# Head of a hybrid diffusion layer: modulation columns in two groups, first token block's features in two groups of four

## What is computed

```python
mod = jnp.dot(jax.nn.silu(cond), w_ada) + b_ada
sh1, sc1, gt1, sh2, sc2, gt2 = [m[:, None, :] for m in jnp.split(mod, 6, axis=-1)]
h = _rmsnorm(x, g_pre_mix) * (1 + sc1) + sh1
z = jnp.einsum('bld,de->ble', h, w_in)
q, k, v, o, ig, fg, u, ga, gb = jnp.split(z, IN_SPLIT_POINTS, axis=-1)
```

## Time and profile before

| | |
|---|---|
| median of 3 runs | 1746.36 us (1746.0 to 1747.34) |
| the profiled execution | 1746.76 us |
| its span | 1744.9 us |
| TensorE busy | 1728.8 us, 99% |
| VectorE, ScalarE, GpSimd busy | 1201.5, 680.1, 266.4 us |
| TensorE's granted clock over the span | 0.997 of full |

### The profile page before, as it was taken

The page is one execution under the profiler, slowest core; times in us unless marked ns, Lnnn a source line. Parts: engine busy times, 40 slices in busy tenths (PEclk is TensorE's granted clock), DMA queues, the critical chain, the costliest instruction groups (busy, mean ns, idle before and its releaser), DMA issues.

```text
span 1744.9 us, 26886 instructions
## 1 busy us (share of the span) xinstructions
PE 1728.8 (99%) x10432; PEld 1626.5 (93%) x10432; DVE 1201.5 (69%) x2547; ACT 680.1 (39%) x1229; POOL 266.4 (15%) x260
## 2 busy tenths in 40 slices
PE   8999999999999999999999999999999999999998
PEld 2998999999999999999988899999999999888887
DVE  4677556566565565364464579888888888798998
ACT  3633221333144143262243454434344444444454
POOL 3010000100000000010000062444433333100000
PEclk9999999999999999999999999999999999999999
DMA  9124334424434455265232331233222222686876
GB/s 346 52 56 141 90 105 128 126 84 145 112 95 159 124 138 185 74 243 170 95 125 94 105 121 66 86 114 110 90 71 72 75 76 76 199 279 221 272 248 246
DMA packets 216275, 236.17 MB, mean 135 GB/s; under 512 B 11568, under 2 KB 160828, under 8 KB 216148
## 3 DMA queue, kind: packets, MB, share of 16 engines
q1 hardware_dynamic: 200916, 179.54, 33.8%
q0 software_dynamic: 10752, 38.00, 6.4%
q10 hardware_dynamic: 4480, 16.91, 2.4%
HBM read 181.49 MB, written 52.92 MB: 134 GB/s over the span
## 4 chain that ended last, share of the span: by engine, by line
PE 90%; DVE 5%; ACT 1%; DMA 1%; issue 1%; SPq 1%; POOL 1%; ACTq 0%; DVEq 0%; POOLq 0%
PE ps L1466 19%; PE ps L1106 13%; PE ps L1107 12%; PE ps L1108 12%; PE ps L1408 6%; PE ps L1483 5%; PE ps L1484 5%; PE ps L1485 5%; PE ps L1273 2%; PE ps L1277 2%; PE ps L1275 2%; PE ps L1289 2%; PE ps L1291 1%; PE ps L1290 1%; DVE mid_g L2647 1%; DVE up_lo L2178 1%
## 5 line engine op out<-in xcount | busy, mean ns | idle before, releaser
L1106 PE MATMUL ps<-H_hi,ring_hi 128*128 128x384 f32 x1200 | 406.5, 339 | 4.7 <-DVE H_lo L2178 4.7
L1107 PE MATMUL ps<-H_lo,ring_hi 128*128 128x384 f32 x1200 | 401.9, 335 | 0.0
L1108 PE MATMUL ps<-H_hi,ring_lo 128*128 128x384 f32 x1200 | 401.8, 335 | 0.0
L1106 PEld LDWEIGHTS ps<-H_hi,ring_hi 128*128 128x128 f32 x1200 | 226.0, 188 | 5.8 <-DVE H_lo L2178 5.5
L1107 PEld LDWEIGHTS ps<-H_lo,ring_hi 128*128 128x128 f32 x1200 | 226.0, 188 | 0.3
L1108 PEld LDWEIGHTS ps<-H_hi,ring_lo 128*128 128x128 f32 x1200 | 225.8, 188 | 0.0
L2355 DVE SCALAR_TENSOR_TENSOR Cst<-Cst,GE,ps 128x257 f32<-128x257 f32 x56 | 26.8, 478 | 163.2 <-PE ps L1277 163.2
L1466 PE MATMUL ps<-T_hi,up_hi 128*128 128x288 f32 x608 | 130.5, 296 | 0.4 <-ACT held_g L2013 0.3
L1466 PE MATMUL ps<-T_hi,up_lo 128*128 128x288 f32 x608 | 130.2, 296 | 0.0
L1466 PE MATMUL ps<-T_lo,up_hi 128*128 128x288 f32 x608 | 130.2, 296 | 0.0
L2178 DVE TENSOR_TENSOR up_lo<-up_raw,up_hi 128x512 fp32r<-128x512 f32 x114 | 89.6, 789 | 57.2 <-ACT up_hi L1971 57.2
(11 more groups left out here) (332 smaller groups left out, 3609.1 us busy)
## 6 DMA issues: line engine op xcount, KB each, us to landing
raw<-in_w_in_dram SPq DMA_DIRECT2D x44, 512.0 KB, 4.1
up_raw<-in_w_up_dram SPq DMA_DIRECT2D x38, 512.0 KB, 5.2
w_raw<-in_w_down_dram SPq DMA_DIRECT2D x66, 256.0 KB, 3.3
raw<-in_w_ada_dram SPq DMA_DIRECT2D x32, 512.0 KB, 5.5
X<-z_f SPq DMA_DIRECT2D x44, 256.0 KB, 3.9
GE<-z_gates SPq DMA_DIRECT2D x72, 128.0 KB, 4.1
w_sub<-in_w_down_dram SPq DMA_DIRECT2D x33, 256.0 KB, 4.0
z_w_diff<-w_raw SPq DMA_DIRECT2D x22, 256.0 KB, 2.5
```

What stands on the lines that cost most here:

```text
L1106: pe.matmul(out, whi, xhi, start=first, stop=False)
L1107: pe.matmul(out, whi, xlo, start=False, stop=False)
L1108: return pe.matmul(out, wlo, xhi, start=False, stop=last)
```

## The change

- `w_ada` columns come as four rows of 512: row 0 is the shift and row 1 the scale of features 0 to 3, rows 2 and 3 those of features 4 to 7. They lie in the memory of `H_hi` and `H_lo`.
- SP's order: first token block, row 0, query unit, row 1 (in four parts), two value units, rows 2 and 3, token blocks 1 and 2. The eleven vectors are issued by ScalarE.
- All eight matmuls of each row are TensorE's. Rows 0 and 1 stand ahead of the first features. TensorE then does four query steps, row 2, the first four value steps of tiles 0 and 1, row 3, two transposes, the columns, the first four value steps of tile 2, four query steps, and the other twelve value steps. The last eight of these take the transposes of the second block.
- Four banks are open at a time: query, and a value tile each in banks 1, 2 and 6. The transposes of the first block have two banks (3 and 4), those of the others three (3, 4, 5).
- The low part of the query unit is VectorE's; the value units' high parts are ScalarE's and their low parts VectorE's. GpSimd has none of them.
- ScalarE evacuates value tile 1 behind the second block's features.

The core of the diff; left out are helper functions renamed or moved, the index of `first_coef` by group, and the loops of blocks 1 and 2, which are as before.

```diff
-    AG = ADA0 * P // 512
-
-    DVE_GROUP, PE_CELLS = 2, 2
-    DVE_CELLS = KD - PE_CELLS
-    ADA_PARTS = (1, 2, 2, 4)
+    FG = 2
+    KG = KD // FG
+    RW = KG * P
+    ADA_PARTS = (1, 4, 2, 2)
...
+    ada_at = [0, 0] + [BW + RW * (g - 1) if FG > 2 else T - RW for g in range(1, FG) for _ in range(2)]
+    ada_home = [place(f"ada_home{s}", [P, KD, T], at=HH0 + 4 * KD * T * s) for s in range(2)]
...
+    def ada_cols_of(r):
+
+        return slice((r % 2) * DM + r // 2 * RW, (r % 2) * DM + (r // 2 + 1) * RW)
+
+    def ada_rows_in(r, ks):
+
+        return ada_home[r % 2][:, ks, ada_at[r]:ada_at[r] + RW]
+
+    def row_out(r):
+
+        return ps[0:2, r % 2 if r < 2 else 5, 0:RW] if RW == 512 or r < 2 else ps[0:2, 5, r % 2 * RW:(r % 2 + 1) * RW]
+
+    def xt_bank(w):
+
+        return 3 + w % 2 if w < KD else 3 + w % 3
...
-            ada_load(0)
-            x_load(0)
-            ada_load(1)
...
-            ada_load(2)
-            ada_load(3)
...
+            x_load(0)
+            ada_load(0)
             for n, it in enumerate(raw_items):
+                if n == 1:
+                    ada_load(1)
                 if n == 3:
+                    for r in range(2, 2 * FG):
+                        if r == 2 * FG:
+                            x_load(1)
+                        ada_load(r)
...
-            hi1, lo1 = split_of(1)
-            pool.tensor_tensor(lo1, raw[:, raw_n(1) % RS, :], hi1, ALU.subtract).then_inc(lo_ready, 1)
-            v_raw, v_hi, v_lo = [[value_part(j, what) for j in range(2)] for what in ("raw", "hi", "lo")]
-            for j in range(2):
-                n = raw_n(2 + j)
-                pool.wait_ge(landed[n % RS], 16 * (n // RS + 1))
-                pool.tensor_copy(v_hi[j], v_raw[j]).then_inc(hi_ready, 1)
-                pool.wait_ge(hi_ready, 2 + j)
-                pool.tensor_tensor(v_lo[j], v_raw[j], v_hi[j], ALU.subtract).then_inc(lo_ready, 1)
...
+                if w >= 2:
+                    pe.wait_ge(xt_free, w - (1 if b == 0 else 2))
+                norm_turn(X0, ps[:, xt_bank(w), :], b, k).then_inc(xt_done, 1)
...
+            def ada_rows(r):
+
+                if r > 2 and (RW == 512 or r % 2 == 0):
+                    pe.wait_ge(row_read, r)
+                for k in range(KD):
+                    if k % (KD // ADA_PARTS[r]) == 0:
+                        pe.wait_ge(ada_part_in(r, k), 16)
+                    mm = pe.matmul(row_out(r), condT[:, :, k], ada_rows_in(r, k), start=(k == 0), stop=(k == KD - 1))
+                mm.then_inc(row_done, 1)
+
+            def ada_cols(group):
+
+                for r in (2 * group, 2 * group + 1):
+                    pe.wait_ge(row_read, r + 1)
+                    for j in range(KG):
+                        at = 2 * (r % 2 * KD + group * KG + j)
+                        mm = pe.transpose(ps[:, 7, at:at + 2], ada_row[:, r, j * P:(j + 1) * P], ident[0:2, 0:2])
+                mm.then_inc(ada_used, ADA0 // FG)
...
             pe.wait_ge(cond_done, 1)
             ada_rows(0)
-            ada_rows(1)
-            ada_rows(DVE_GROUP, 0, PE_CELLS, PE_CELLS)
             pe.wait_ge(vectors_in, 16 * 11)
             pe.transpose(ps[:, 7, 0:92], vecs[0:92, 0, :], ident[0:92, 0:92])
             pe.transpose(ps[:, 7, 92:180], vecs[0:88, 1, :], ident[0:88, 0:88])
             pe.transpose(ps[:, 7, 180:268], vecs[0:88, 2, :], ident[0:88, 0:88]).then_inc(vec_done, 1)
             pe.wait_ge(x_scaled, TB)
-            for k in range(4):
-                first_norm(0, k)
+            first_norm(0, 0)
+            first_norm(0, 1)
+            ada_rows(1)
             pe.wait_ge(vec_done, 2)
-            ada_cols(0, 0)
-            ada_cols(1, 8)
-            ada_rows(3, 0, 4)
-            ada_group_sum()
-            ada_cols(DVE_GROUP, 2 * ADA0).then_inc(ada_used, ADA0 // 2)
-            ada_rows(3, 4, KD)
-
-            for b in range(NB):
-                if b == 0:
-                    pe.wait_ge(lo_ready, 2)
+            ada_cols(0)
+
+            tiles_of = [[(j, k) for j in range(TB) for k in range(KG * g, KG * (g + 1))] for g in range(FG)]
+            turn_steps = tiles_of[FG - 1][-KD:]
+            turns = {step: range(KD * n // len(turn_steps), KD * (n + 1) // len(turn_steps)) for n, step in enumerate(turn_steps)}
+            for g in range(FG):
+                for k in range(KG * g, KG * (g + 1)):
+                    if k == 0:
+                        pe.wait_ge(lo_ready, 2)
+                    mm = ramp_query(0, k)
+                    if k + 2 < KD and (k + 2) // KG == g:
+                        first_norm(0, k + 2)
+                if g == FG - 1:
+                    mm.then_inc(done0, 1)
+                else:
+                    ada_rows(2 * g + 2)
+                for j, k in tiles_of[g]:
+                    if (j, k) == (0, 0):
+                        pe.wait_ge(lo_ready, 4)
+                    if j == TB - 1 and k == KG * g and g < FG - 1:
+                        ada_rows(2 * g + 3)
+                        for n in range(2):
+                            first_norm(0, KG * (g + 1) + n)
+                        ada_cols(g + 1)
+                    if g == FG - 1:
+                        for n in turns.get((j, k), ()):
+                            if n == 0:
+                                pe.wait_ge(x_scaled, 2 * TB)
+                            first_norm(1, n)
+                    mm = ramp_value(j, (1, 2, 6)[j], k)
+                    if k == KD - 1:
+                        mm.then_inc(done0, 1)
+
...
+            vecA = [b_ada[0], g_pre_mix[0], g_post_mix[0], g_pre_ffn[0], g_post_ffn[0],
+                    g_head[0].rearrange("h v -> (h v)"), pool_scale[0]]
+            at = 0
+            for v in vecA:
+                n = v.shape[0] // P
+                act.dma_start(vecs[at:at + n, 0, :], v.rearrange("(r p) -> r p", p=P)).then_inc(vectors_in, 16)
+                at += n
+            for j, o, v in ((1, 0, conv_w[0, 0]), (1, 44, conv_w[0, 1]), (2, 0, conv_w[0, 2]), (2, 44, conv_b[0])):
+                act.dma_start(vecs[o:o + 44, j, :], v.rearrange("(r p) -> r p", p=P)).then_inc(vectors_in, 16)
...
             hi_split(1)
+            row_copy(1)
             act.wait_ge(coef1, 1)
-            first_evac(0, range(0, 3))
+            first_evac(0, range(0, 2))
+            value_hi(0)
+            first_evac(0, range(2, 4))
+            value_hi(1)
+            row_copy(2)
             row_copy(3)
-            first_evac(0, range(3, 4))
             act.wait_ge(coef1, 2)
             first_evac(0, range(4, KD))
             x_stats(1)
             query_evac(0)
             value_evac(0)
+            first_evac(1)
             value_evac(1)
-            first_evac(1)
             value_evac(2)
...
             scale_x(0)
-            dve.wait_ge(cond_done, 1)
-            ada_group(PE_CELLS, KD)
+            lo_split(1)
             dve.wait_ge(vec_done, 2)
             first_coef(0)
...
-            norm_split(0, tsc, 4, 0, range(0, 3), direct=False)
+            norm_split(0, tsc, 4, 0, range(0, 2), direct=False)
+            value_lo(0)
+            norm_split(0, tsc, 4, 0, range(2, 4), direct=False)
+            value_lo(1)
             first_coef(1)
-            norm_split(0, tsc, 4, 0, range(3, KD), direct=False)
+            norm_split(0, tsc, 4, 0, range(4, KD), direct=False)
             scale_x(1)
             norm_split(0, tsc, 4, 1, direct=False)
             scale_x(2)
```

More of the change, by code:

```diff
@@ L512, in build @@
     staged = list(stage_no)
-    ROW_BANK = (0, 1, 2, 1)
     NORM_AFTER = (2, 5, 8)
@@ L1139, in first_norm @@
                 w = b * KD + k
-                if w >= 4:
-                    pe.wait_ge(xt_free, w - 3)
-                norm_turn(X0, ps[:, 3 + w % 4, :], b, k).then_inc(xt_done, 1)
-            def ada_rows(g, k0=0, k1=KD, last=KD):
-                if g == 3 and k0 == 0:
-                    pe.wait_ge(row_read, 2)
-                for k in range(k0, k1):
-                    if k % (KD // ADA_PARTS[g]) == 0:
-                        pe.wait_ge(ada_part_in(g, k), 16)
-                    mm = pe.matmul(ps[0:2, ROW_BANK[g], :], condT[:, :, k], adaw[:, g, k, :], start=(k == 0), stop=(k == last - 1))
-                if k1 == last:
-                    mm.then_inc(row_done, 1)
@@ L1156, in ada_cols @@
-            def ada_cols(g, at):
-                pe.wait_ge(row_read, g + 1)
-                for j in range(4):
-                    mm = pe.transpose(ps[:, 7, at + 2 * j:at + 2 * j + 2], ada_row[:, g, j * P:(j + 1) * P], ident[0:2, 0:2])
-                return mm
-            def ada_group_sum():
-                pe.wait_ge(ada_mac, 2 * DVE_CELLS)
-                pe.wait_ge(pool_seq, 7)
-                for a in range(4 * DVE_GROUP, 4 * DVE_GROUP + 4):
-                    for cond in range(2):
-                        pe.matmul(ps[:, 7, 2 * a + cond:2 * a + cond + 1], group_part[:, cond, (a % 4) * P:(a % 4 + 1) * P],
```

(31 more changed lines are left out.)

85 lines of the change are left out of this document (31 added, 54 removed).

## The result

The changed kernel took 1763.23 us (median of 4 runs, 1762.41 to 1763.8), the kernel before 1746.63 on the same chip: ratio 1.0095 [1.0077, 1.0112], 16.6 us slower. The forecast was 1761.8 in a range of 1755.5 to 1766. The profiled execution took 1762.41 us, its span is 1760.6, so 15.7 us more than the span of before.

The account below looks back on a forecast made before the run. TensorE bounds. Work without waits 61.9 plus waits 10.4 puts the second block's query product at 72.3, 9.7 us later; clock falls add 5.7. So 15.4 us on the median 1746.36 give 1761.8, range 1755.5 to 1766.

Parts of the forecast that it names:

- What bounds, and that delays go through: TensorE, busy 1728.8 of 1744.9 us, bounds; any shift of the second block's query product (62.64 us) reaches the end.
- The floor (later start, more work): Head: start 14.0 instead of 9.53, work 47.9 instead of 44.7 us; second block at 61.9 without waits.
- first fall: Gap 8.05 to 14.0 us, ahead of row 0: the clock falls to half, costing 2.3 us.
- Waits: TensorE's new waits in the head make 10.4 us, putting the second block's query product at 72.3.
- x wait: Before the second block's transposes TensorE stands 3.3 us for scaled x, ready at 66.6.
- The clock: Three emptied stretches of the head: falls costing 2.3, 1.7 and 1.7 us, together 5.7, bounds 0 and 7.
- third gap: Stretch 57 to 66.6 us, with 5 us of work: a fall of the clock likely, taken at 1.7 us.
- the casts: First block's features: VectorE's casts take 0.35 us instead of 2.52 once GpSimd's splits are gone.
- A: Clock does not fall in the second and third stretch, or in none: sum 9.7 to 12 us, chance 0.2.
- B: Not slower: columns fill TensorE's waits, new waits under 0.7 us; 1744.1 with early landing, chance 0.03.
- C: Row 0 or 1 held 3 to 5 us, first query step at 38 again: sum 18 to 21, chance 0.1.
- D: One cover counted as gone holds (x scaled early, or later query steps closer): 10.4, about 1757, chance 0.07.

Follow-up runs that it names:

- experiment 3: Changed kernel with six of row 3's eight products back on VectorE and their sum on TensorE: 1759.9 us, ratio 1.0075.
- Experiment 4: Changed kernel with only the transfer order undone, first columns loaded ahead of the token block: 1763.93 us, ratio 1.0099.
- experiment 5: Changed kernel with first columns loaded ahead of the token block and row 1 ahead of the transposes: 1760.06 us, ratio 1.0077.
- after: The changed kernel itself, with the whole change, against the kernel before: 1763.23 us, ratio 1.0095.
- experiments 2: Changed kernel with seven unused matmuls filling TensorE's gap ahead of the first column product: 1760.78 us, ratio 1.0078.
- experiment 6: Changed kernel with GpSimd's five weight splits put back, ScalarE's and VectorE's taken out: 1766.14 us, ratio 1.0108.
- experiment 7: Kernel before with GpSimd's weight splits moved to ScalarE and VectorE, nothing else changed: 1744.45 us, ratio 0.9987.
- Experiment 8: Changed kernel with second block's x scaled early, six row 3 products on VectorE, first columns loaded first, row 1 ahead of transposes: 1751.6 us, ratio 1.0026.
- experiment 9: Kernel before without GpSimd's splits, second high half behind the last evacuation, first low half behind feature 3: 1744.38 us, ratio 0.9981.

## Why the prediction was right, and where it was not

**What bounds, and that delays go through: right.** 14.66 us at the second block are 15.7 at the end; nothing behind absorbed them. The last 1.0 us, later waits that grew from 0.8 to 1.2 and from none to 0.6, was not forecast; it is no larger than what such waits differ by between the profiles of these kernels.

**The floor (later start, more work): right in size.** Start 14.37 for 14.0. The more of work was put at 5.1 less 1.95; the rows of experiment 3 give 3.3 us for it, its median 3.9.

**But the cause of the late start was half named.** The forecast put it down to the order of the transfers. Experiment 4 undoes this alone and gains nothing; experiment 5 needs row 1 ahead of the transposes as well, and gets 3.7 us (4.75 in the profile) of the 6.8 that the forecast had for late start and first fall together. Whether TensorE's order alone would do was not tried. Read for a time, the step held; read as advice, it would have misled.

**Waits: right one by one, the sum a little low.** First query step 35.28 (34.8 forecast with the clock); row 2 at 41.08 (40.95 with both falls in it); fifth query step 62.44 (61.55); x wait 2.88 (3.3); the eight steps behind it at 0.71, as forecast. With the two falls of this profile, 2.17 and some 1.4, the forecast's own steps give 72.3 + 3.5 = 75.8 for the landmark, and it was at 77.30: 0.4 by the start and 1.1 us mis-sized. The 1.1 is a sum of small ones. From the end of row 1 to the first query step it takes 3.8 us (3.6 forecast), from the second half's column transposes to the fifth query step 2.8 (2.45), from there to the last four value steps 4.6 (4.25), for these 1.7 (1.5), and rows 2 and 3 with the steps between them lose another 0.4 by rounding; the x wait gives 0.4 back. The first two are the same chain: the forecast allowed 2.5 us from the last column transpose to the query step, for durations that add up to 2.2, and the trace has 2.6 in the first group (32.65 to 35.28) and 2.8 in the second (59.68 to 62.44).

**The clock: mechanism right, number of falls not fixed.** 2.3 forecast for the first, 2.17 measured (9.20 less 7.03). The second was put at 1.7; from the first query step to row 2 it takes 5.80 us instead of the forecast's 4.45, so 1.35 if all of the difference is the clock. The third was put at 1.7 and cost nothing in the profile of after; in experiments 2, 3 and 6 it cost 1.6. So the 5.7 us were 3.5 in this execution, and about 5 in those with a third fall. In the profile the handovers and the late waits made up for the missing fall, and this is why 15.4 and 15.7 lie so close: that closeness is luck, errors of some 2 us each way cancel. One reading behind these terms was off as well. The forecast has the clock of the kernel before fall after two waits, of 2.15 and of 1.83 us. In the trace the clock is at 0.67 on the mean from 43.0 to 43.3, and the second wait begins at 43.4: the fall came while TensorE worked, behind the first wait alone. The statement of the Trainium skill (TensorE: Matmul & The Clock Gate, "What's actually happening"), that the low clock is the default, by which the first fall was certain, agrees with the trace at 12 us and with the return to 1.00 at 19; for the third gap it settles nothing, since the clock held there in three profiles (after, 4 and 5) and fell in three others (2, 3 and 6).

**GpSimd: only the casts were seen.** The forecast had them fall from 2.52 to 0.35, which is so. In the changed order the casts would come behind GpSimd's work anyway; what the splits would hold is the coefficients, 1.55 us in experiment 6 (2.1 on the medians). And in the kernel before, almost half of what the splits cost came by way of the clock (experiment 7), which the forecast did not tie to the splits. The Trainium skill (SBUF — State Buffer, "Who interferes with whom") tells of an exclusive lock on the ports that VectorE and GpSimd share; the 1.72 us of an 8-element operation that ends 0.03 us behind GpSimd's subtraction agree with it.

**Rivals.** A (no second or third fall) is out as put, since the second is in the profile; the third is missing in some executions. B (not slower) is out: the start came at 14.37 and the new waits made 9.10 us, where 0.7 was its point. C (first features not earlier) is out: 35.28 against 38.43. D (a cover holds) is out: the x wait is there with 2.88 us.

**What remains of the whole.** On the medians, each good to some 2 us, the 16.6 us are: 4.2 the late scaling of x, 3.9 the group on TensorE, 3.7 the order of columns and transposes, 0.7 more when all three go together, and 4.1 left. In these 4.1 the gain from GpSimd (1.5 to 3.0 us) is counted already, so the split into two groups should cost some 5.5 to 7 us by itself; this is an estimate, no kernel has that part alone. Experiment 8's waits (7.9 us idle) are its likely place. They were not taken apart further.

## What to carry over

Beginning a piece of work earlier gains only if the engine that bounds had been waiting for just that; here TensorE's cover for later steps (the value steps of the second block's x) was spent to fill a gap at the front. When a trial like this fails, test its parts on the old kernel: one of them, the splits taken off GpSimd, was worth 3.0 us by itself. And undo order edits on all queues together, the transfers and the engine's own order: the transfers alone gained nothing here (experiment 4). Shorter waits can also come with a fall of the clock less, as in experiment 7, so look at the granted clock before putting a gain down to the waits.

## What the runs showed of the hardware

- A VectorE operation on 128x8 took 1.72 instead of 0.17 us beside a GpSimd subtraction (experiment 6), so not only large casts (2.52 against 0.35) are held. Two additions with one operand in `ps` took 0.24 us together beside the same subtraction, as without it.
- The clock fell in gaps of 6.62 us (after) and 4.90 us (experiment 4), and after a thinly filled stretch. In the third gap it differed: behind waits of 2.88 us it stayed at 1.00 in the profiles of after, 4 and 5, and behind 2.86, 2.86 and 2.87 us it fell to 0.50 in those of 2, 3 and 6. The first fall's price differed too: row 0 took 8.43 to 9.82 us where it takes 7.03 at 1.00.
- It also fell with TensorE busy for 5.00 of 5.00 us (experiment 9, 0.66), behind 16 small matmuls of one column. The same instructions ran at 1.00 in experiment 7. Why it fell is open.
- The clock is not all of the spread: the four highest times of experiment 7, 1745.92 to 1747.16 us against a median of 1744.45, have mean granted clocks of 0.999 and 1.000. What made them longer is open.
